# A chain of small VectorE instructions in attention, cut into three pieces in three steps of the tile

## The reference, cut to what matters

```python
h = layer_norm(x)
attn = bidir_block_attention(q, k, v)              # 8 query heads of 64
merged = concat(rms_norm(attn, attn_out_g), rms_norm(lru, lru_out_g))
h = layer_norm(DEEPNORM_ALPHA * h + merged @ w_out, ln1_g, ln1_b)
logits = h @ router_weights + bias                 # 20 columns; then a mixture of 16 experts
```

## Time and profile before

| what | value |
|---|---|
| median of 3 runs | 1675.6 us (1673.4 to 1678.62) |
| the profiled execution's own time | 1674.68 us |
| its span, first to last instruction | 1673.0 us |
| PE busy | 1500.4 us, 90% |
| DVE busy | 1104.0 us, 66% |
| ACT busy | 906.6 us, 54% |
| POOL busy | 491.2 us, 29% |
| mean granted TensorE clock | 0.943 |

### The profile page before, as it was taken

The page is one execution under the profiler, slowest core; times in us unless marked ns, Lnnn a source line. Parts: engine busy times, 40 slices in busy tenths (PEclk is TensorE's granted clock), DMA queues, the critical chain, the costliest instruction groups (busy, mean ns, idle before and its releaser), DMA issues. The chain is left out here.

```text
span 1673.0 us, 29904 instructions
## 1 busy us (share of the span) xinstructions
PE 1500.4 (90%) x9130; PEld 1305.4 (78%) x9131; DVE 1104.0 (66%) x2101; ACT 906.6 (54%) x1527; POOL 491.2 (29%) x345
## 2 busy tenths in 40 slices
PE   6999989999897999999999999985799999999940
PEld 6999967777686899989999899981577788777830
DVE  8788539999737877777777777777453433444237
ACT  4444447878646655655555555632464544555325
POOL 1221125666510011111111111120445353454318
PEclk9999999999957999999999999995799999999975
DMA  8865443344334121111221121116689677786566
GB/s 277 310 218 216 166 153 139 139 177 164 113 130 158 45 72 63 57 57 62 78 71 57 57 69 64 45 42 223 198 245 279 187 221 194 209 259 182 111 203 261
DMA packets 124006, 249.58 MB, mean 149 GB/s; under 512 B 22291, under 2 KB 75539, under 8 KB 123925
## 3 DMA queue, kind: packets, MB, share of 16 engines
q1 hardware_dynamic: 93984, 160.97, 27.8%
q0 software_dynamic: 12528, 45.62, 11.8%
q10 hardware_dynamic: 17412, 41.96, 6.5%
HBM read 153.98 MB, written 94.54 MB: 149 GB/s over the span
## 5 line engine op out<-in xcount | busy, mean ns | idle before, releaser
L1681 DVE TENSOR_TENSOR d_probs_t_lo<-d_pt_ps,d_probs_t_hi 128x512 fp32r<-128x512 f32 x256 | 164.4, 684 | 92.1 <-ACT d_probs_t_hi L1608 91.6
L1831 POOL TENSOR_TENSOR d_h_tile<-d_s_tile,d_ln_g_b 128x512 f32<-128x512 f32 x30 | 38.8, 1292 | 566.9 <-ACT d_s_tile L1629 538.0
L1608 ACT ACTIVATE d_probs_t_hi<-d_pt_ps 128x512 fp32r<-128x512 f32 x256 | 139.2, 596 | 113.9 <-PE d_pt_ps L1487 107.5
L1657 DVE TENSOR_REDUCE d_neg_max<-d_s_ps 128x1 f32<-128x1024 f32 x128 | 155.4, 1214 | 2.9 <-PE d_s_ps L1476 2.9
L114 PE MATMUL acc<-k_hi,wl_hi 128*128 128x256 f32 x512 | 146.0, 285 | 4.5 <-DVE k_lo L570 4.5
L1487 PE MATMUL d_pt_ps<-ident,d_probs 128*128 128x128 f32 x1024 | 135.4, 275 | 12.7 <-DVE d_probs_t_lo L1681 9.9
L114 PE MATMUL e_a_ps<-up_hi,e_xt_hi 128*128 x336 | 138.6, 413 | 8.9 <-issue 4.6
L1591 ACT ACTIVATE d_probs<-d_s_ps,d_neg_max 128x1024 f32<-128x1024 f32 x128 | 143.4, 1120 | 3.9 <-DVE d_neg_max L1657 3.9
L115 PE MATMUL acc<-k_lo,wl_hi 128*128 128x256 f32 x512 | 144.8, 283 | 0.0
L116 PE MATMUL acc<-k_hi,wl_lo 128*128 128x256 f32 x512 | 144.7, 283 | 0.0
L1505 PE MATMUL d_ot_ps<-d_probs_t_hi,d_v_split 128*128 128x256 f32 x512 | 127.7, 287 | 9.9 <-DVE d_probs_t_lo L1681 9.9
(11 more groups left out here) (404 smaller groups left out, 4107.4 us busy)
## 6 DMA issues: line engine op xcount, KB each, us to landing
up_raw<-in_exp_w SPq DMA_DIRECT2D x32, 1024.0 KB, 10.0
down_raw<-in_exp_w SPq DMA_DIRECT2D x16, 1024.0 KB, 11.7
d_h_tile<-h_dram SPq DMA_DIRECT2D x16, 522.0 KB, 3.5
h_dram<-v_all ACTq DMA_DIRECT2D x16, 512.0 KB
ht_hi_dram<-k_hi ACTq DMA_DIRECT2D x8, 1024.0 KB, 4.3
ht_lo_dram<-k_lo ACTq DMA_DIRECT2D x8, 1024.0 KB, 6.7
q_dram<-wq_raw ACTq DMA_DIRECT2D x16, 512.0 KB, 2.7
d_q_tile<-q_dram SPq DMA_DIRECT2D x16, 512.0 KB, 3.8
```

What stands on the lines that cost most here:

```text
L1608: act.activation(pt_hi[:, c * HALF:(c + 1) * HALF, h % 2], pt_ps[c][:], ACT.Copy).then_inc(pth_done[c], 1)
L1657: dve.tensor_reduce(nm[:, u, h:h + 1], s_ps[h % 2][:], AX, ALU.max, negate=True).then_inc(nm_done, 1)
L1681: dve.tensor_tensor(pt_lo[:, part, h % 2], pt_ps[c][:], pt_hi[:, part, h % 2].bitcast(F32), ALU.subtract)\
L1831: pool.tensor_tensor(h1[:, part], s_t[u][:, part], g_b[:, part], ALU.mult).then_inc(hg_done, 1)
```

## The change

`rsqrt` is divided into `rsqrt_guess` (three instructions) and `rsqrt_steps` (nine), and `norm_chain` into `norm_start` and `norm_end`. Of the 18 instructions, the first six (statistics, scalings, guess) stay in step 1. The nine Newton instructions and `shift1` go into step 2, behind `add_lru`. The two of `route_rows` go into step 3, behind `add_attn`. ACT's normalisation goes from step 2 to step 4; POOL's and SP's lists are as before, and wait for it. No instruction is added or taken away. The order behind the last tile is as before.

```diff
--- before.py
+++ after.py
@@ -91,11 +91,18 @@
 
 
 def rsqrt(dve, link, x, y, t, wide=False):
-
+    rsqrt_guess(dve, link, x, y, t)
+    rsqrt_steps(dve, link, x, y, t, wide)
+
+
+def rsqrt_guess(dve, link, x, y, t):
 
     link(dve.tensor_scalar(t.bitcast(I32), x.bitcast(I32), 1, None, ALU.logical_shift_right))
     link(dve.tensor_scalar(y.bitcast(I32), t.bitcast(I32), -1.0, float(0x5F3759DF), ALU.mult, ALU.add))
     link(dve.tensor_scalar(x, x, -0.5, None, ALU.mult))
+
+
+def rsqrt_steps(dve, link, x, y, t, wide=False):
     for _ in range(NEWTON):
         if x.shape[-1] == 1 and not wide:
             link(dve.scalar_tensor_tensor(t, y, x, y, ALU.mult, ALU.mult))
@@ -1624,7 +1631,7 @@
                     act.activation(m_hi[:, 0:FT], m_ps[:].rearrange("p (k t) -> p k t", k=FT), ACT.Copy)\
                        .then_inc(mh_done, 1)
                     act.activation(junk[:], o_n[:], ACT.Square, accum_out=ssa[:]).then_inc(ssa_done, 1)
-                if h == 2 and late:
+                if h == 4 and late:
                     act.wait_ge(ln_done, t - 1)
                     act.activation(s_t[u][:, 0:D], s_t[u][:, 0:D], ACT.Identity, bias=shift1[:], scale=rr[:, 1:2]).then_inc(xn_done, 1)
                 if h == 7:
@@ -1650,6 +1657,8 @@
             LRU_LINKS = 2 + RSQRT_LINKS_WIDE
             EARLY = LRU_LINKS + 1 + RSQRT_LINKS_WIDE
             LINKS = 5 + RSQRT_LINKS_WIDE
+            GUESS = 3
+            START = 3 + GUESS
 
             def neg_max(t, u, h):
                 n = NQ * t + h
@@ -1713,7 +1722,7 @@
                 dve.nop(nofuse=True)
                 dve.bn_stats(stats[:, 6 * half:6 * half + 6], s_t[t][:, 512 * half:512 * half + 512]).then_inc(stats_done, 1)
 
-            def norm_chain(link, t, u, post, late):
+            def norm_start(link, t, post, late):
                 if late:
                     dve.wait_ge(stats_done, 2 * (t - 1))
                     dve.nop(nofuse=True)
@@ -1725,11 +1734,17 @@
                 if late:
                     dve.wait_ge(xn_done, t - 1)
                 some = slice(0 if post else 1, 2)
-                rsqrt(dve, link, var[:, some], rr[:, some], tmp[:, some], wide=True)
+                rsqrt_guess(dve, link, var[:, some], rr[:, some], tmp[:, some])
+
+            def norm_end(link, t, post, late):
+                some = slice(0 if post else 1, 2)
+                rsqrt_steps(dve, link, var[:, some], rr[:, some], tmp[:, some], wide=True)
                 if late:
                     dve.tensor_scalar(shift1[:], mv[:, 0:1], rr[:, 1:2], -1.0, ALU.mult, ALU.mult).then_inc(ln_done, 1)
-                    dve.wait_ge(ln_done, t - 1)
-                    route_rows(link, t - 2, u)
+
+            def links_of(t, late, done):
+
+                return Chain(dve, dve_link, (EARLY + LINKS * (t - 2) if late else LRU_LINKS) + done)
 
             def route_rows(link, t, u):
 
@@ -1766,8 +1781,10 @@
                         dve.wait_ge(mh_done, t)
                         dve.tensor_tensor(m_lo[:, 0:FT], m_ps[:].rearrange("p (k t) -> p k t", k=FT),
                                           m_hi[:, 0:FT].bitcast(F32), ALU.subtract).then_inc(m_free, 1)
-                    if post or late:
-                        norm_chain(Chain(dve, dve_link, EARLY + LINKS * (t - 2) if late else LRU_LINKS), t, u, post, late)
+                    if post:
+                        norm_start(links_of(t, late, 0), t, post, late)
+                if h == 2 and post:
+                    norm_end(links_of(t, late, START if late else 1 + GUESS), t, post, late)
                 if h in (3, 5, 6) and post:
                     cut = (3, 5, 6).index(h)
                     dve.wait_ge(m_done, use)
@@ -1775,6 +1792,9 @@
                     if cut:
                         dve.wait_ge(m_free, use)
                         half_stats(1 - u, cut - 1)
+                if h == 3 and late:
+                    dve.wait_ge(ln_done, t - 1)
+                    route_rows(links_of(t, late, LINKS - 2), t - 2, u)
                 if h == 7:
                     dve.wait_ge(yh_done, t + 1)
                     dve.tensor_tensor(m_lo[:, FT:KD], yt[:], m_hi[:, FT:KD].bitcast(F32), ALU.subtract).then_inc(yl_done, 1)
@@ -1791,7 +1811,10 @@
             dve.tensor_tensor(m_lo[:, 0:FT], m_ps[:].rearrange("p (k t) -> p k t", k=FT),
                               m_hi[:, 0:FT].bitcast(F32), ALU.subtract).then_inc(m_free, 1)
             link = Chain(dve, dve_link, EARLY + LINKS * (t - 2))
-            norm_chain(link, t, 0, True, True)
+            norm_start(link, t, True, True)
+            norm_end(link, t, True, True)
+            dve.wait_ge(ln_done, t - 1)
+            route_rows(link, t - 2, 0)
             dve.wait_ge(lru_proj, 3)
             add_lru(t, 0, 2, last_out[2]).then_inc(sum_made, 1)
```

## The result

The changed kernel took 1653.19 us, the median of 4 runs (1650.26 to 1657.61), against 1674.5 for the kernel before in the same comparison; the ratio is 0.9867, 95% interval 0.9842 to 0.9892. The profiled execution took 1657.61 us, its span is 1655.9. Over more runs (six of the changed kernel, 23 of the one before) it was 1655.96 against 1675.24, ratio 0.9875 (0.985 to 0.990). So it is faster, as forecast, by 19 to 21 us instead of 16.

A forecast was written before the change was run, and what follows sets the result against it. PE was taken to bound the kernel. 1.30 us won less 0.15 of new waiting, 1.15 us a tile over 14 tiles, gave 16.1 us: 1659.5 us against the median, range 1655.5 to 1667.5.

The forecast's parts named there:

- PE sets the pace, and loses 1.34 us in steps 2 and 3: Steady attention: PE busy 483.1 of 498 us; late DVE work costs it 0.91 + 0.43 us a tile.
- Step 1 with six instructions frees lo(2): DVE's `probs_t_lo` of step 2 can begin 2.82 us earlier, leaving PE's step 3 transposes no wait, 1.4 us to spare.
- The bank of step 3: `add_lru` frees it at 788.28, step 3's projection wants it at 788.99: the 6.5 us wait goes, by 0.7 us.
- lo(3) at T(3) + 3.00, and 0.15 us of new waiting: DVE's `probs_t_lo` of step 3 begins 3.00 us behind PE's step 3 transposes; PV waits 0.15 us, bounds 0 and 0.27.
- 1.30 us a tile to be won: PE's mean loss per late tile in attention; over 14 tiles, 18.2 us as all that can be won.
- The range: Whole kernel: 1655.5 to 1667.5 us, taking in gains of 14.4 to 18.8, 2 us run spread and the first rival.
- The hidden moves: ACT's normalisation, `route_rows`, POOL, stores and load of h at later places cost nothing; the load hidden by 5 us.
- `norm_o` beside POOL: DVE's `norm_o` of step 4 while POOL works: loss taken as 0, bounds 0 and 0.4 us.
- The rivals: Three alternatives: POOL holds `norm_o` with lo(3) at upper bound, 1666.8 us, 12%; wait only moves, 5%; cold links, 3%.
- The moved wait: Rival: `probs_t_lo` of step 3 comes 1.15 us later than reckoned and PV waits instead: 1675.6 us, 5%.
- cold links: Rival: each of nine links of DVE's resumed chain costs 0.21 us more; slower, 1686.1 us, 3%.

The follow-up runs named there:

- route_only: The kernel before with only the two `route_rows` instructions moved to step 3: 1660.11 us, ratio 0.9909.
- pad3: The changed kernel with three more linked two-column DVE instructions behind step 2's Newton instructions: one run, attention stage 615.2 us.
- pad6: The changed kernel with six more linked two-column DVE instructions behind step 2's Newton instructions: 1675.86 us, ratio 0.9991 to the kernel before.
- after_again: The changed kernel run once more without edit, against the kernel before: 1655.96 us, ratio 0.9875.
- beside_pool: The changed kernel with six more linked two-column DVE instructions in step 5 of late tiles, while POOL works: one run, attention stage 609.2 us.
- turn7b: The changed kernel with PE's third turning back moved to step 7 and DVE's second half-statistics behind step 7's maximum: 1650.24 us, ratio 0.9860 to the kernel before.
- act_only: The kernel before with ACT's normalisation alone moved to step 4, POOL's and SP's work following: 1676.57 us, ratio 1.0003.
- two_pieces: The changed kernel with `route_rows` left behind the Newton instructions in step 2: 1665.06 us, ratio 0.9935 to the kernel before.
- id_step2: The changed kernel with ACT's normalisation back in step 2: 1680.58 us, ratio 1.0034 to the kernel before.

## Why the prediction was right in kind and off in size

**PE sets the pace, and loses 1.34 us in steps 2 and 3.** Right: in each of the 14 tiles both steps are as long as their undisturbed twins.

**Step 1 with six instructions frees lo(2).** Right: T(2) + 1.43 for 1.41 reckoned. route_only shows that with 16 instructions left in step 1 0.23 and 0.19 us are lost there in two tiles of 14 (step 2 4.38 and 4.34), and nothing in the others.

**The bank of step 3.** Right, the 6.5 us entry is gone; with room to spare, since `add_lru` came earlier than reckoned.

**lo(3) at T(3) + 3.00, and 0.15 us of new waiting.** This is the step that failed. It began at T(3) + 2.58, and nothing waits; 0.3 us are to spare, by pad3 and pad6. Two terms were too large. I took `add_lru` to start 0.50 us behind T, from step 0; in step 2 it is 0.20. Step 0's is still at 0.50 in the changed kernel (778.39 against 777.89). Two things stand ahead of it there and not in step 2: `norm_o`, and waits for two more semaphores. The kernel before had a row that parts them, in step 4, with `norm_o` ahead but without the two waits:

```profile
798.56 0.57 DVE L1747 SCALAR_TENSOR_TENSOR d_s_tile<-d_m_ps,d_lru_rstd,d_h_tile 128x348 f32<-128x348 f32 x1
```

That is T(5) + 0.25, so most of the 0.30 us goes with the two waits, though no run takes them out. And from `shift1` to lo it was 0.13, my lower end, not 0.25: I had measured the 0.25 on an instruction that a link makes the next one wait for, while nothing makes lo wait for `shift1`. The right row would have been one without a link behind it. Together 0.30 + 0.12 = 0.42 us, the whole way from 3.00 to 2.58.

**1.30 us a tile to be won.** 18.5 us over 14 tiles are 1.32. With the 0.15 that was not lost (2.1 us in 14 tiles) this gives the stage: 16.1 forecast, 18.5 measured, within the 14.4 to 18.8 that I had as bounds.

**The range.** It began at 1655.5, and 1653.19 lies below. (By its own terms it should have begun at 1675.6 - 18.8 - 2 = 1654.8, which doesn't take in 1653.19 either.) Against the forecast of 1659.5, 6.3 us are missing: 2.4 are the stage's, 1.1 the kernel before, whose median was 1674.5 with one more run, and 2.8 lie outside attention. So the wait of 0.15 alone, at nothing, would have left the result outside: 1675.6 - 18.2 = 1657.4. The second term that failed is the 2 us for the spread of the runs: 23 runs of one and the same kernel lay between 1670.6 and 1682.6. The rest outside attention, untouched in all these kernels, took from 1040.4 to 1056.5 us in the profiled executions. It varies in two stages, and in both the longer one has the lower granted clock. The expert stage of the changed kernel, in its first profile and in after_again's:

```profile
1171.00:1603.90 432.90, 404.88 (x1932) 327.31 (x1932) 167.13 (x357) 217.01 (x343) 189.09 (x116) 0.98 0.75 209
```

```profile
1165.20:1605.80 440.60, 410.06 (x1932) 330.79 (x1932) 166.95 (x359) 216.78 (x343) 189.12 (x116) 0.97 0.75 205
```

432.9 us at 0.98 and 440.6 at 0.97. The clock isn't all of it: PE's busy time differs by 5.2 of the 7.7 us, and its waits for DVE's `e_hid` are 5.3 us instead of 3.1. In pad3 the same stage took 446.7 us at 0.96, and there a second cause shows. Three DVE instructions with two SBUF inputs, at 1210.7, 1401.8 and 1525.2, took 6.0 us, where the 13 others of their line took 1.23. This is the first, with the two POOL instructions behind which it was held:

```profile
1210.72 6.05 DVE L2251 TENSOR_TENSOR down_lo<-down_raw,down_hi  x1 [1.89 <-ACT down_hi L2431]
```

```profile
1210.71 2.63 POOL L2244 TENSOR_TENSOR up_lo<-up_raw,up_hi  x1
...
1213.04 2.63 POOL L2251 TENSOR_TENSOR down_lo<-down_raw,down_hi  x1
```

It ends at 1216.77, 1.1 us behind the second. In these three POOL started first, by 0.01 to 0.10 us; in the 13 others DVE did, by 0.04 us or more, and wasn't held. Together the three took 14.3 us more of DVE's time; how much of that reached the stage's length wasn't measured. One such instruction was held in pad6 (3.48 us) and one in beside_pool (6.18), none in the other ten profiles. The stage ahead of attention, in the changed kernel and in turn7b:

```profile
248.90:517.40 268.50, 248.07 (x1299) 202.12 (x1297) 208.71 (x251) 184.82 (x304) 126.46 (x92) 0.88 0.38 138
```

```profile
250.40:511.70 261.30, 241.40 (x1297) 195.89 (x1297) 212.60 (x251) 184.70 (x304) 125.86 (x92) 0.90 0.39 142
```

268.5 at 0.88 and 261.3 at 0.90. The medians differ by more than the stage's 18.5 us, by 2.8 in the first comparison and 0.8 in the second, and that is within this scatter; that it is chance is the likeliest reading, and it wasn't shown by itself.

**The hidden moves.** Right: ACT, `route_rows`, POOL, the stores and the load of h cost nothing; act_only shows it alone.

**`norm_o` beside POOL.** The cost, nothing, was right; my reason for it wasn't tested. `norm_o` took 0.43 us, for 0.42 before, but it started at 795.95 and POOL at 795.99, and in all 14 tiles it was first, by 0.04 to 0.24 us. What a `norm_o` does that starts while POOL runs, no run shows, so the right number may be luck. `add_lru`, at 796.28, did start while POOL ran, and took 0.57 as without it.

**The rivals.** None occurred. The moved wait became real in two_pieces, 10 us of it; cold links didn't show (0.194 us a link in the second piece). The way to be slower that an experiment found was another, id_step2.

## What to carry to other kernels

A chain of small instructions on an engine that isn't the bound costs only the part by which the next instruction in that engine's list comes too late: here 0.91 us behind a chain of 4.13, and 0.43 more one step on through `add_lru`. Two of 18 instructions moved would have brought two thirds of the gain. Before a piece is put elsewhere, reckon for each engine's list what stands behind it there and when that is due, to a tenth of a microsecond, and take each gap from a row with the same waits around it. What the piece's consumers wait for has to move along: ACT's move, worth nothing alone, decided the sign.

## What the runs showed of the hardware that I had not expected

A two-column `tensor_scalar` with one SBUF input is held by a running POOL `tensor_tensor` (1.14 us instead of 0.16), a one-column one isn't (0.14 to 0.155, 42 times); an instruction with two SBUF inputs is held on one column too (0.825 to 1.159 us, 14 times), and so is one on 20 columns (1.17 to 1.23 us instead of 0.24, 14 times in route_only). A DVE instruction that starts ahead of POOL's isn't held (13 of 16 in pad3, the nearest by 0.04 us), so a hold can come and go from execution to execution: `down_lo` of the expert stage took 1.23 us in ten of the 13 profiles throughout, and 6.0 in three of its 16 places in pad3. The length of two stages that the change doesn't touch varied by 7 and 8 us between profiles without such an instruction (261.3 to 268.5 and 432.2 to 440.6 us), the longest at a lower granted clock than the shortest (0.88 against 0.90, 0.97 against 0.98).
